# First expert pair interleaved with the token gather, its weight tiles reloaded in quarters

## The reference, cut to what matters

```python
# pg_top, g_sel: best of 4 groups; pe_top, e_sel: best 2 of its 8 experts
w = pg_top * pe_top / sum(pe_top)                       # one weight for each choice
combine = sum(one_hot(eid, 32) * w[..., None], axis=1)  # (256, 32)
hid = silu(einsum('td,edf->tef', t, w1)) * einsum('td,edf->tef', t, w3)
hid = hid * combine[..., None]
out = einsum('tef,efd->td', hid, w2)                    # added to x
```

## Time and profile before

| | us |
|---|---|
| median of 3 runs (lowest, highest) | 1231.69 (1230.03, 1232.03) |
| the profiled execution's own time | 1229.87 |
| its span, first to last instruction | 1228.1 |
| PE busy / DVE busy / ACT busy / POOL busy | 1185.8 / 696.1 / 373.9 / 45.8 |
| mean DMA rate over the span | 274 GB/s |

### The profile page before, as it was taken

The page is one execution under the profiler, slowest core; times in us unless marked ns, Lnnn a source line. Parts: engine busy times, 40 slices in busy tenths (PEclk is TensorE's granted clock), DMA queues, the critical chain, the costliest instruction groups (busy, mean ns, idle before and its releaser), DMA issues.

```text
span 1228.1 us, 18911 instructions
## 1 busy us (share of the span) xinstructions
PE 1185.8 (97%) x7298; PEld 893.7 (73%) x7298; DVE 696.1 (57%) x1021; ACT 373.9 (30%) x396; POOL 45.8 (4%) x60
## 2 busy tenths in 40 slices
PE   8999999999999999999999999999999999999995
PEld 8888888888888888888898888555555455445552
DVE  5687545544666667566886656544444444443443
ACT  4544433334344354544343442110010110000103
POOL 1000000001002020100000000000000000000002
PEclk9999999999999999999999999999999999999998
DMA  8566555665555554556576595899999999999994
GB/s 281 186 190 205 172 181 175 191 189 188 171 171 161 162 162 153 159 164 203 175 269 182 172 388 195 339 430 431 431 431 431 432 431 432 431 432 431 428 420 192
DMA packets 152619, 336.64 MB, mean 274 GB/s; under 512 B 10992, under 2 KB 135040, under 8 KB 138112
## 3 DMA queue, kind: packets, MB, share of 16 engines
q1 hardware_dynamic: 148000, 335.68, 73.3%
q10 hardware_dynamic: 4576, 0.37, 0.3%
HBM read 333.93 MB, written 2.11 MB: 274 GB/s over the span
## 4 chain that ended last, share of the span: by engine, by line
PE 83%; DMA 13%; DVE 1%; ACT 1%; issue 1%; SPq 0%; POOL 0%; ACTq 0%; POOLq 0%; DVEq 0%
PE ps L927 20%; PE ps L1228 14%; DMA w_b<-in_w_dram 12%; PE ps L956 11%; PE ps L929 10%; PE ps L958 6%; PE ps L1255 5%; PE ps L1099 4%; PE ps L1100 2%; PE ps L1264 2%; PE ps L1265 1%; PE ps L1183 1%; DMA xin<-in_x_dram 1%; PE ps L914 1%; PE ps L1205 0%
## 5 line engine op out<-in xcount | busy, mean ns | idle before, releaser
L1344 DVE TENSOR_TENSOR wsplit<-wraw,wsplit 128x2048 fp32r<-128x2048 f32 x120 | 277.1, 2309 | 183.0 <-ACT wsplit L659 182.2
L927 PE MATMUL ps<-act_split,wsplit 128*128 128x512 f32 x1024 | 362.4, 399 | 0.0
L659 ACT ACTIVATE wsplit<-wraw 128x2048 fp32r<-128x2048 f32 x120 | 230.1, 1917 | 386.4 <-PE ps L929 203.4
L929 PE MATMUL ps<-act_split,wsplit 128*128 128x256 f32 x1024 | 286.8, 280 | 0.0
L1228 PE MATMUL ps<-w_a,xe_a 128*64 128x256 f32 x960 | 221.3, 384 | 10.2 <-DMA w_b<-in_w_dram 10.0
L927 PEld LDWEIGHTS ps<-act_split,wsplit 128*128 128x128 f32 x1024 | 192.2, 188 | 48.0 <-issue 1.8
L1228 PE MATMUL ps<-w_b,xe_b 128*64 128x256 f32 x960 | 221.3, 384 | 0.0
L956 PE MATMUL ps<-wsplit,act_split 128*128 128x512 f32 x608 | 216.3, 400 | 0.0
L1228 PEld LDWEIGHTS ps<-w_a,xe_a 128*64 128x64 f32 x960 | 128.0, 138 | 97.4 <-issue 21.2
L929 PEld LDWEIGHTS ps<-act_split,wsplit 128*128 128x128 f32 x1024 | 193.3, 189 | 0.2
L958 PE MATMUL ps<-wsplit,act_split 128*128 128x256 f32 x608 | 170.4, 280 | 0.0
(11 more groups left out here) (310 smaller groups left out, 1086.0 us busy)
## 6 DMA issues: line engine op xcount, KB each, us to landing
wraw<-in_w_in_dram SPq DMA_DIRECT2D x88, 1024.0 KB, 5.0
w_a<-in_w_dram SPq DMA_DIRECT2D x39, 2048.0 KB, 15.3
w_b<-in_w_dram SPq DMA_DIRECT2D x39, 2048.0 KB, 19.6
wraw<-in_w_out_dram SPq DMA_DIRECT2D x16, 1024.0 KB, 5.1
w_a<-in_w_dram SPq DMA_DIRECT2D x15, 1024.0 KB, 14.4
w_b<-in_w_dram SPq DMA_DIRECT2D x15, 1024.0 KB, 17.9
wraw<-in_w_branch_m_dram SPq DMA_DIRECT2D x8, 1024.0 KB, 5.1
wraw<-in_w_branch_a_dram SPq DMA_DIRECT2D x8, 1024.0 KB, 5.1
```

The costliest lines, as they stand in the source:

```text
L659: act.activation(wsplit[:, q % 2, :, 0], wraw[:, q % RAW], ACT.Copy).then_inc(rounded, 1)
L927: pe.matmul(banks[b], w[:, k, 0, b * P:(b + 1) * P], a, start=first and k == 0, stop=False)
L929: last = pe.matmul(banks[b][:, 0:T], w[:, k, 1, b * P:(b + 1) * P], a[:, 0], start=False, stop=last_half and k == HALF_K - 1)
L1344: dve.tensor_tensor(wsplit[:, q % 2, :, 1], wraw[:, q % RAW], wsplit[:, q % 2, :, 0].bitcast(F32), ALU.subtract).then_inc(split, 1)
```

## The change

- TensorE gathers with five banks (3 to 7) in place of eight. `by_most`, with its branch, comes after the first five chunks instead of after all 16; the other chunks are gathered inside the branch.
- The first pair's hidden parts are cut into quarters of four chunks. w1 quarters 0, 1 and 2 are done right after gather chunks 5, 9 and 13; then chunks 14 and 15; then w3 quarter 0, w1 quarter 3 and w3 quarters 1 to 3.
- Each quarter (semaphore `first_used`, or `h_parts` for the last of each matrix) lets SP reload the same quarter with pair 1's weights: 16 loads of 512 KB in place of 8 of 1 MB.
- DVE computes `starts` and `most` before the token weights. The token weights (7 small instructions) come after the first `xe_first` copy, the mix after the second, and `make_x2` after `gate(0)` instead of before `slots(0)`. `xe_first` is copied in four pieces.
- Zeroing the padding columns of `xg` goes from DVE to POOL, ahead of the routing chain's end. ACT waits for the full x2 only before it writes `ys_hi`.

```diff
 def gather_bank(c):
-    return (c + 2) % 8 if c < 14 else c - 12
+    return 3 + c % AHEAD                      # AHEAD, QUARTER = 5, 4
...
# SP
-                for part in range(PARTS):
-                    parts_done(1, part)
+                def pair_1_quarter(w, q):
                     for b in range(2):
-                        load_part(b, 2 + b, part)
+                        load_steps(b, 2 + b, w, q * QUARTER, (q + 1) * QUARTER, w13_loaded[w][q // 2] if q % 2 else w13_first[w])
...
+                    for n, (w, q) in enumerate(((0, 0), (0, 1), (0, 2), (1, 0))):
+                        sp.wait_ge(first_used, n + 1)
+                        pair_1_quarter(w, q)
+                    parts_done(1, 1)
+                    pair_1_quarter(0, 3)
+                    for n, q in ((5, 1), (6, 2)):
+                        sp.wait_ge(first_used, n)
+                        pair_1_quarter(1, q)
+                    parts_done(1, 3)
+                    pair_1_quarter(1, 3)
                 next_rows(2, 0)
...
# TensorE
-                for c in range(8):
-                    if t == 0 and c == 6:
-                        pe.wait_ge(rank_read, 1)
+                for c in range(AHEAD):
                     gather(c, t)
...
+            def first_quarter(w, q):
+                if w == 0:
+                    pe.wait_ge(xg_act, (q + 1) * QUARTER // 2)
+                    pe.wait_ge(xg_dve, (q + 1) * QUARTER // 2)
+                    if q < 3:
+                        pe.wait_ge(xe_first_ready, q + 1)
+                    else:
+                        pe.wait_ge(xe_ready, 2)
+                pe.wait_ge(w13_loaded[w][q // 2], 32)
+                for k in range(q * QUARTER, (q + 1) * QUARTER):
...
+            def first_hidden():
+                for q, end in ((0, 6), (1, 10), (2, 14)):
+                    gather_chunks(end - QUARTER if q else AHEAD, end)
+                    first_quarter(0, q)
+                turn_mix(0)
+                gather_chunks(14, DC)
+                first_quarter(1, 0)
+                first_quarter(0, 3)
+                for q in range(1, 4):
+                    first_quarter(1, q)
...
# DVE, experts(1)
-                gathered(1, EARLY)
-                dve.tensor_copy(xe_first[:, 0:EARLY], xg[:, 0:EARLY, ds(second, SLOTS)]).then_inc(xe_ready, 1)
-                gathered(EARLY + 1, DC)
-                dve.tensor_copy(xe_first[:, EARLY:], xg[:, EARLY:, ds(second, SLOTS)]).then_inc(xe_ready, 1)
-                make_mix(0, 0, 0)
-                make_x2()
+                for q in range(4):
+                    gathered(q * QUARTER + 1, (q + 1) * QUARTER)
+                    ks = slice(q * QUARTER, (q + 1) * QUARTER)
+                    copy = dve.tensor_copy(xe_first[:, ks], xg[:, ks, ds(second, SLOTS)])
...
+                    if q == 0:
+                        weights()
+                    if q == 1:
+                        make_mix(0, 0, 0)
                 slots(0, 0)
                 gate(0)
+                make_x2()
                 up(0)
```

More of the change, by code:

```diff
@@ L53 @@
 WARM_ROUTE, WARM_SELECT = 18, 6
-EARLY = 12
+AHEAD, QUARTER = 5, 4
 HALF_LEAD, NO_LEAD = 5, 8
@@ L517, in next_rows @@
                         load_rows(slot, b, ds(i * 2 + b, 1))
-                for part in range(PARTS):
-                    parts_done(1, part)
+                def pair_1_quarter(w, q):
                     for b in range(2):
-                        load_part(b, 2 + b, part)
+                        load_steps(b, 2 + b, w, q * QUARTER, (q + 1) * QUARTER, w13_loaded[w][q // 2] if q % 2 else w13_first[w])
+                if chunks > 1:
+                    for part in range(PARTS):
+                        w, h = divmod(part, 2)
+                        parts_done(1, part)
+                        for q in (2 * h, 2 * h + 1):
+                            pair_1_quarter(w, q)
+                else:
+                    for n, (w, q) in enumerate(((0, 0), (0, 1), (0, 2), (1, 0))):
+                        sp.wait_ge(first_used, n + 1)
+                        pair_1_quarter(w, q)
+                    parts_done(1, 1)
[5 more added lines that the diff above has]
+                    pair_1_quarter(1, 3)
                 next_rows(2, 0)
@@ L1189, in _, with gather_chunks @@
                 pe.wait_ge(sel_ready, t + 1)
-                for c in range(8):
-                    if t == 0 and c == 6:
-                        pe.wait_ge(rank_read, 1)
+                for c in range(AHEAD):
                     gather(c, t)
[L1194 to L1197, removed]
+            def gather_chunks(first, end):
+                for c in range(first, end):
+                    pe.wait_ge((xg_act, xg_dve)[(c - AHEAD) % 2], (c - AHEAD) // 2 + 1)
+                    for t in range(TT):
+                        gather(c, t)
             def turn_mix(s):
@@ L1208, in hidden @@
             def hidden(i, s, operands, between=((), (), (), ())):
-                first = operands[1] is xe_first
-                if not first:
-                    pe.wait_ge(xe_ready, s * 2 + 2)
+                pe.wait_ge(xe_ready, s * 2 + 2)
                 pe.wait_ge(hid_ready, s + 1)
@@ L1234, in hidden @@
                         more()
+            def first_quarter(w, q):
[4 more added lines that the diff above has]
+                        pe.wait_ge(xe_first_ready, q + 1)
+                    else:
+                        pe.wait_ge(xe_ready, 2)
+                pe.wait_ge(w13_loaded[w][q // 2], 32)
+                for k in range(q * QUARTER, (q + 1) * QUARTER):
+                    for b, rows_of in enumerate((xg[:, :, 0:SLOTS], xe_first)):
+                        last = pe.matmul(ps[b * SLOTS:(b + 1) * SLOTS, 2 * w, 0:FF], rows_of[:, k], w13[b][:, w, k],
+                                         start=k == 0, stop=k == DC - 1)
+                if q < 3:
+                    last.then_inc(first_used, 1)
+                else:
+                    last.then_inc(h_parts, 2)
+            def first_hidden():
[8 more added lines that the diff above has]
+                    first_quarter(1, q)
             def turn(s):
@@ L1285, in pair_in_chunks @@
                             scatter(s, 0, range(GROUPS_OUT))
+                    gather_chunks(AHEAD, DC)
                     pair_in_chunks(0, 0, 0)
+                    for w in range(2):
+                        pe.wait_ge(w13_first[w], 64)
                     with pe.Fori(0, N_PAIRS // 2 - 2) as j:
@@ L1294, in experts @@
                     return
-                hidden(0, 0, (xg[:, :, 0:SLOTS], xe_first))
+                first_hidden()
                 turn(0)
                 rows(0, 0, 0)
+                for w in range(2):
+                    pe.wait_ge(w13_first[w], 64)
                 def hidden_and_scatter(i, half, order=((0, 1), (2, 3), (4, 5), (6, 7))):
@@ L1793, in _ @@
                                          ALU.is_equal, ALU.add).then_inc(sel_ready, 1)
[L1795 to L1802, removed]
+            dve.wait_ge(rank_read, 1)
             dve.tensor_reduce(stat[:, 35:36], table[:, 0], AX.X, ALU.max)
@@ L1809, in _, with weights @@
             dve.tensor_copy(most_i[:], stat[0:1, 35:36]).then_inc(tab_ready, 1)
-            dve.memset(xg[:, :, PAIRS:], 0.0)
             steps_x = Steps(dve, dve_x)
+            def weights():
+                dve.wait_ge(gexp_done, 2)
+                steps_x.done(dve.tensor_scalar(sc[:, W_1], sc[:, E_EXP], 1.0, None, ALU.add))
+                steps_x.done(dve.tensor_tensor(sc[:, W_1], sc[:, W_1], sc[:, GSUM], ALU.mult))
+                steps_x.done(dve.reciprocal(sc[:, W_1], sc[:, W_1]))
+                steps_x.done(dve.tensor_tensor(sc[:, W_2], sc[:, W_1], sc[:, E_EXP], ALU.mult))
+                steps_x.done(dve.tensor_tensor(wt[:], oh[:, :, 0], by_token(W_1, EXPERTS), ALU.mult))
+                steps_x.done(dve.tensor_tensor(rt[:, 3], oh[:, :, 1], by_token(W_2, EXPERTS), ALU.mult))
+                steps_x.done(dve.tensor_tensor(wt[:], wt[:], rt[:, 3], ALU.add))
             def starts_of(i, c, experts=(0, 1)):
```

17 lines of the change are left out of this document (12 added, 5 removed).

## The result

| | median us (runs) | ratio to before, 95% interval |
|---|---|---|
| before, in the same sessions | 1230.91 (20) | |
| changed | 1233.45 (20) | 1.0020 (1.0014 to 1.0026) |
| changed, measured again (e0) | 1233.15 (12) | 1.0019 (1.0007 to 1.0031) |

The change costs 2.5 us, where 0.6 was forecast. The new median lies inside the forecast range, 1.1 us above the 1232.3 named; it would have lain 1.9 above had the forecast started from the median of 20 runs (1230.91) and not from that of the first 3 (1231.69). The profiled span went from 1228.1 to 1230.5.

What follows compares the result with a forecast made beforehand. From the gather on, the weight stream was taken to bound the kernel. Stream -0.3 plus delay of pair 0's end 0.9 gave +0.6 us, from 1231.69 to 1232.3; range 1228.5 to 1235.5.

Steps and rivals of the forecast that it cites:

- the signs that I had named for a wrong forecast: w2 issued before 791, no hole ahead of it, or gather plus first pair over 2 us above 38.9.
- The stream, and that it restarts at w2 of pair 2: Queue empties before pair 2's w2 load; restart costs 1.8 us, so almost nothing of the 11 us earlier start is left.
- D: Delay of pair 0's end, forecast 0.9 us (0.2 to some 2.8); the stream was to change by D - 0.3.
- The end of pair 1's w1/w3: Pair 1's w1/w3 loads were to end at about 790 instead of 793.7, after 1.8 + 12.2 us from 776.1.
- Rival C: Quarter loads run under 370 GB/s, the queue never runs dry and the old time, 1231.7 us, stays; 6%.
- Handovers: Three more changes between gather and expert products on TensorE, 0.05 us each, together 0.15, up to 0.45.
- Waits for `xe_first`: TensorE waits for the gathered pieces' read-out and copy before the quarters, 0.3 us, between 0 and 0.9.
- Rival B: Five-bank read-out sets the pace; each of four boundaries pays the 1.3 us chain, 5.2 us, giving 1237.2; 14%.
- `make_x2` ahead of `hid`: On DVE, `make_x2` between gate and `hid` starts `hid` late, 0.45 us, between 0.2 and 0.7.
- The clock: TensorE's granted clock was 1.00 in all stretches read, so it was not the subject and had no term.
- The memset on POOL: Memset moved from DVE takes about 1.0 us beside routing, costing nothing, up to 1.0 if it holds up that chain.
- Rival A: Pair 1's w1/w3 ending 3.7 us earlier carries to the end, 1228.0, as the skill's interleaving rule suggests; 12%.

Runs made afterwards that it cites:

- e0: The changed kernel measured again, unaltered, as the control of the follow-up set; median 1233.15 us, ratio to before 1.0019.
- e2: Changed kernel, but the two long additions of the full x2 stand ahead of the slots again, as before; ratio to before 1.0005.
- e6: Kernel before plus 24 unused identity matmuls between pair 0's transposes and its w2 products, a pure delay; ratio to before 1.0029.
- e10: Kernel before plus 8 unused identity matmuls ahead of pair 0's w2 products, a shorter pure delay; ratio to before 1.0029.
- e3: Kernel before with each 1 MB load of pair 1's w1/w3 issued as two of 512 KB; TensorE also waited for both matrices' even quarters; ratio 1.0025.
- e7: Changed kernel, but SP waits for the fourth quarter's release before issuing any load of pair 1; ratio to before 1.0073.
- e4: Changed kernel with halves in place of quarters, 1 MB loads for pair 1 and the full x2 made ahead of the slots; ratio to before 0.9995.
- e5: e4 with w2 of pair 2 in two column halves and pair 2's w1/w3 in four loads per expert, released by part; ratio to before 0.9983.
- e11: The same kernel as e5, measured once more; ratio to before 0.9999.

## Why the prediction was right, and where it was not

The median is inside the range, and the mechanism held. The size did not: 0.6 was forecast and 2.5 measured, at the edge of what I had called no change. And one of the signs that I had named for a wrong forecast came: gather and first pair took over 2 us more than 38.9, namely 2.56 more in the profile and 3.32 in e0.

**The stream, and that it restarts at w2 of pair 2: right.** The streams follow TensorE's releases and not the first load. Where w2 of pair 2 is one load issued into an empty queue, D - 0.3 gives 2.3, 3.0, 1.4 and 4.5 (the changed kernel, e0, e2, e6); the streams were 2.1, 2.9, 1.4 and 4.3 late. The restart itself, forecast at 1.8, cost 1.4 to 1.6. In e10 the sum fails (0.9 against 2.4), for the reason given there, and it does not apply to e3 and e7, where a later wait of TensorE sets the stream.

**The end of pair 1's w1/w3, forecast 790.1: too early by 3.4.** The last five quarters went from 778.18 to about 793.5, 15.3 us instead of 1.8 + 12.2 = 14.0, at 366 GB/s from 780 to 790. The other 2.1 us are the later issue (776.1 was forecast). The hole was there all the same, but only 1.5 us wide. Rival C's condition, a rate under 370 GB/s, was met; what it foretold, a queue that never runs dry, failed only because pair 0 ended 2.6 us later too. So that the hole came as forecast is in part luck: two errors of the sum, 3.4 us in the loads' end and 2.0 in the w2 issue (792.5 forecast, 794.46 measured), cancel for the greater part. e3 had loads of the same size at 416 GB/s, so the size alone does not explain the low rate; what does is open.

**D: this is the term that was mis-sized, 0.9 against 2.56 in the profile.** By parts:
- Handovers (TensorE's changes between gather and expert products), forecast 0.15, measured 1.07 in e0, where the clock was full: gather 6.00 + 4.08 + 4.10 + 2.00 = 16.18 against 15.49, expert products 14.52 against 14.14. I had counted three more changes of TensorE's work at 0.05. There are six more (seven against one), three return trips at 0.36; the bound that I took from the earlier trace rows, 0.15 for one change, would have given 0.9 had I counted both directions. In e4 one more return trip cost 0.12 in all, so the price is not a constant. The blocks of e0 narrow it down: the two gather blocks of 16 records that follow a quarter directly took 4.08 and 4.10 us, where 3.87 is the pace of the kernel before; the block behind the mix's transposes took 2.00 for 1.94, and e4's one return, behind the same transposes, 5.82 for 5.81. Why the direct return costs more is open.
- Waits for `xe_first`, forecast 0.3: at most 0.14, the gap at quarter 0, which the chain calls issue; there is none at the other quarters. Rival B's price did not come.
- `make_x2` ahead of `hid`, forecast 0.45: 0.5. In the trace of the changed kernel it ends at 785.59, and `hid` starts on its heels; e2 took it away.

```profile
781.10 4.49 DVE L1884 TENSOR_TENSOR x<-x2hi,x2lo 128x2048 f32<-128x2048 f32 x2
785.63 0.66 DVE L1927 SCALAR_TENSOR_TENSOR hid<-ps,slot_both,sg 128x256 f32<-128x256 f32 x1
```

- The clock, which I had called no subject because the earlier trace rows have it at 1.00, and so put at nothing in the sum: 0.9 us at the gather's start in one profile and 1.7 at the w2 products in the other. The first, in the stretches of the changed kernel:

```profile
752.00:756.00 4.00, 4.00 (x15) 3.37 (x14) 3.17 (x14) 0.00 (x0) 0.00 (x0) 0.60 0.93 393
756.00:760.00 4.00, 3.89 (x17) 3.57 (x17) 1.99 (x5) 2.07 (x3) 0.00 (x0) 1.00 0.15 66
```

Without the clock D is 1.7 and the sum -0.3 + 1.7 = 1.4, with it 2.3 to 3.0. The timed runs say how much of this they have, since each lists its mean granted clock, and a run is the longer the lower it is. At 0.994 the runs of the changed kernel (e0's with them, 32 in all) took 1232.7 us in the mean and those of the kernel before (92, from the same sessions as the experiments) 1231.2; at 0.993 it was 1234.0 and 1232.3. So at an equal clock the change costs 1.4 to 1.7 us. The mean clock was 0.9938 against 0.9944; at 0.8 to 1.0 us for each 0.001 that is another 0.5 to 0.6 (an estimate from these runs). Where in a timed run the clock fell is not on record, nor is it shown that the change makes it fall.

**The memset on POOL: right.** It took 0.95 us, and the way from the last x2 to the first `sel` was 12.6 us in both.

```profile
744.75 0.95 POOL L655 MEMSET xg<- 128x1024 f32 x1
```

It had ended (745.70) before the first DVE instruction of the form that the Trainium skill ("SBUF — State Buffer", Who interferes with whom) names, at 745.84. So the trace does not contradict the lock that this section describes, and does not show it.

**Rival A and the rule beside it.** The interleaving of the Trainium skill ("Perfetto Trace Analysis", Optimization Strategy) was carried out, and brought nothing by itself. The same section goes on to look for what blocks the gaps on the engine that one optimizes for; carried over to this stream of loads that is the next release, and it was the useful half.

## What to carry to other kernels

When a stream of loads is the bound, list every release that it depends on, with the work queued at each: an earlier start is worth only what it leaves at the tightest of them, and a consumer that becomes later there costs nearly its whole delay. Count the work that the interleaving adds to the releasing engine, in both directions of each change, before the time that it frees. Once one release is eased, look at the next one before building it.

## What the runs showed of the hardware that I had not expected

- A queue need not be empty to lose time: with 1.15 us of work in hand at the issue (e10) the rate fell to 315 GB/s for 5 us, with 2.1 us (before) it did not fall. Over all traces 0.7 to 1.8 us in hand lost 0.3 to 1.4 us, and 2.7 or more at most 0.3.
- TensorE going to and fro between the gather (512 columns, fp32r) and the 256-column float32 products cost 0.36 us for each return trip in the mean of e0, the changed kernel at full clock, and 0.12 in e4.
- The granted clock fell to its lower level for some microseconds in places that differ between executions of one program (e5 and e11, the changed kernel and e0), each after TensorE had waited, in e5 2.6 us, in e0 1.3 and 0.5, and on the path this cost 0.9 to 1.7 us, in e7 3.1. At the start of the gather it did so in 4 of the 10 kernels with the changed routing end (changed, e2, e7, e11) and in none of the 4 with the old one. Whether that is chance is open.
